# Edges between the stages of a two-block transformer kernel: what is split ahead, in which order tiles are summed, and where query blocks stand

## The chip, the cores and the metric

The kernel runs on one core of a Trainium2 chip. The metric is the device time of one execution in microseconds (us), the median of several runs. Five engines with a queue each work side by side and wait for each other by semaphores: TensorE (PE), VectorE (DVE), ScalarE (ACT), GpSimd (POOL), and SyncE (SP), which issues DMAs.

## The reference

Input x is one sequence of 512 tokens with 1024 features, all in fp32. The kernel holds it transposed, as 8 blocks of 128 features (partitions) by 512 tokens.

```python
# first block: gated linear attention and retention, 8 heads each
h = rms_norm(x, norm_g) * (1 + scale) + shift
m = sigmoid(ga) * uA + sigmoid(gb) * uB          # from h @ w_in, "mixed" in the kernel
x = rms_norm(x + gate * (m @ w_out), final_g)
# second block
def conformer_conv(x):
    a = glu(x @ w_pw1 + b_pw1)                   # 2048 columns
    y = depthwise_conv(a, w_dw, 31 taps, causal) + b_dw
    y = silu(layernorm(y, ln_g, ln_b))
    return y @ w_pw2 + b_pw2
h = x + conformer_conv(rmsnorm(x, norm_mix[0]))
h = h + swiglu_ffn(rmsnorm(h, norm_ffn[0]), up[0], down[0])
kv = rmsnorm(h, norm_kv) @ w_kv                  # 4 key/value heads of 64
q = rmsnorm(h, norm_mix[1]) @ w_q                # 16 heads, window of 128
h = h + banded_sink_attention(q, k, v, sinks, rel_bias) @ w_o
h = h + swiglu_ffn(rmsnorm(h, norm_ffn[1]), up[1], down[1])
out = rmsnorm(h, norm_final)
```

## The kernel before

**Dense layers.** Every weight matrix is cut into tiles of 1024 x 128 (one output block of 128 features). A tile is 512 KB. Tiles come in one long stream through four slots (`SLOTS`): SP loads tile n into `w_raw` (L429) when the low part of tile n-4 is made; ScalarE writes the high part `w_hi` (L557, `w_high`); GpSimd writes the low part `w_lo` = raw - high (L490, `w_low`). Inputs are split in the same way into `x_hi` and `x_lo`. Per block k of the input TensorE does three matmuls of 128x128 by 512: high with high, `w_hi` with `x_lo`, `w_lo` with `x_hi` (`dense`, L1445 to L1447), 24 a tile, into one PSUM bank of `gps`. The norm's factor is applied behind the matmul, so that a dense layer can start before the norm is known.

**Phases in order:** four pairs of heads (`pairs`, a hardware loop), `w_out`, `pw1` (16 tiles), the convolution, the layer norm, `pw2`, feed-forward 0, `kv`, `q` with the attention, `w_o`, feed-forward 1. `ahead(I, j)` on ScalarE makes the high part of the tile three further on than tile (I, j).

**w_out.** The last pair ends with `mix(0)` and `mix(1)` on VectorE, which write blocks 6 and 7 of `mixed` (L1185, L1187). ScalarE copies the 8 blocks to `xa_hi` (L741), GpSimd makes the low parts of blocks 0 and 1 (L503), VectorE those of 2 to 7 (L1218). `dense_behind` runs the first tile: 16 matmuls with the high input (L1457, L1458), then 8 with the low one (L1461). VectorE then expands the packed taps (`packs`, L1227).

**Residuals.** `residual` on VectorE, for each of 8 tiles: read tile c from PSUM and add it to `res` (L1252, L1254 or L1256), then add square c-1 into the running sum `lnv` (L1242; in w_out also a second sum into `hbuf`, L1245), then write low part c-1 of the next layer's input (L950). ScalarE's `residual`: the next high weight part (`ahead`), then for tile c the high part of the input (L586), the square (L759), in w_out a second, scaled square (L761). The sum over features is taken by TensorE with a matrix of ones: `sum_running` (L1506, L1507, in w_out also L1509, L1510), called behind the first tile of the next phase, at the end of the kernel behind the last tile. Behind w_out it gives two norms, since the first block's last norm and the second's first follow each other: ScalarE L768 to L774, VectorE L1272 and L1274 (`both_ready`).

**pw1 and the convolution.** VectorE scales each pair of tiles and gates them (`halves_in`, `gate`); it adds most taps (L1296), GpSimd 37 of them (L519) from ScalarE's products (L792), and TensorE does the last three chunks from packed taps (L1739) when SP has copied shifted rows (`spread`, L460). During pw1 ScalarE's queue also writes the relative bias to DRAM (L777, 3 MB). In the order of the programs, GpSimd waits for `both_ready` before the low part of pw1's tile 3, and ScalarE makes its high part in the loop over pw1.

**Layer norm.** TensorE adds up the means (`add_to_mean`, L1730), VectorE centers (L1328), ScalarE squares into two buffers in turn (L576), TensorE sums each square (L1500), two matmuls a sum; then ScalarE's logarithm and exponential (L581, L582), VectorE's scaling (L937), ScalarE's Silu in full precision (L830) and into `xa_hi` (L831), VectorE's low part (L943). `dense_abreast` starts pw2 on four tiles at once (L1472, L1473, L1478).

**Attention.** For each pair of heads c: scores (L1804), the minimum and exponential (L1387, L895), scaled probabilities (L1399), their transposes `band_probs(c, e)` (L1814), copies to `pT` (L881, L882), values (L1826). Between them TensorE does the query tile c+2 in parts of blocks (`queries`), and in the last two rounds parts of w_o's first three tiles (`out_part`). The output's high part is L887, its low part L1404.

Of the kernel before, what the change touches and what calls it, by code (L numbers as in the profile page):

```python
# [23 lines left out]
P = 128  # L24
T = 512
# [111 lines left out]
FIRST_LOW = 2  # L137
# [32 lines left out]
def program(nc, weights, ada_in, c_in, xT, x_turned, vec_in, sinks_in, rel_in, ret_tab, lvl_in, eye_in, tri_in, hot_in, ident_in, taps_in,  # L170
            rel_scratch, outT):
    ctx = ExitStack()
    with ctx:
# [68 lines left out]
        at_r = sb("at_r", [P, 2, 10 * P], where=first)  # L242
        first.close()
# [90 lines left out]
        m_hi = sem("m_hi")  # L334
        m_lo = sem("m_lo")
# [16 lines left out]
        center_done = sem("center_done")  # L352

# [47 lines left out]

        products = [hbuf[:, 0, :], hbuf[:, 1, :], hbuf[:, 2, :], sq[:, 0, :], sq[:, 1, :]]
# [79 lines left out]
        def _(pool):  # L482
            TT = nc.gpsimd.tensor_tensor
            for j in range(SLOTS):
                pool.sem_inc(lo_ready[j], 1)

# [9 lines left out]
            with pool.Fori(0, PAIRS) as p:  # L496
                for c in range(SLOTS - 1, PAIR_CHUNKS + SLOTS - 1):
                    if c not in GATE_CHUNKS:
                        w_low(p * (PAIR_CHUNKS // SLOTS) + (START["pairs"] + c // SLOTS), c % SLOTS)

            for c in range(FIRST_LOW):
                pool.wait_ge(m_hi, c + 1)
                TT(xa_lo[:, c, :], mixed[:, c, :], xa_hi[:, c, :].bitcast(F32), ALU.subtract).then_inc(m_lo, 1)  # L503
# [4 lines left out]
            for j in range(3):  # L508
# [17 lines left out]
            for n in range(3, 2 * KC):  # L526
# [15 lines left out]
            w_low(START["pw2"], 2)  # L542
            w_low(START["pw2"], 3)
# [6 lines left out]
        def _(act):  # L550
# [215 lines left out]
            residual("w_out", RMS_FIRST, lambda c: conv_gain[:, c:c + 1], xb_hi, lambda c: vcol("final_g", c))  # L766
            act.wait_ge(sum_done, SUMS[RMS_FIRST])
# [148 lines left out]
        def _(dve):  # L916
# [15 lines left out]
            def x_build(src, gain, hi, lo):  # L932
# [8 lines left out]
                for c in range(KC):  # L941
                    dve.wait_ge(xh_ready, KC * X_PW2 + c + 1)
# [291 lines left out]
            def residual(phase, n, scale=None, shift=None, build=None, double=False):  # L1234
# [13 lines left out]
                for c in range(KC):  # L1248
                    I, j = START[phase] + c // SLOTS, c % SLOTS
                    b = full(I, j)  # L1250
# [7 lines left out]
                    if c >= 2:  # L1258
# [779 lines left out]
```

## Time and profile before

| | |
|---|---|
| Median of 3 runs | 1688.26 us (1686.38 to 1688.56) |
| Profiled execution | 1689.8 us, its span 1688.0 us |
| Busy in the span | PE 1636.1, DVE 803.5, ACT 730.7, POOL 706.5 us |
| Mean granted TensorE clock | 0.989 |

The span goes from the first to the last instruction of the core. Times in the rows are us from its start. "Busy" counts the time in which an engine executes; the idle time of an engine that nobody waits for costs nothing.

### The profile page before, as it was taken

The page shows a single profiled execution, that of the slowest core. Times are in us where ns is not written, and L with a number is a line of the kernel's source. Part 1 is how long each engine was busy: PE and PEld are TensorE (multiplying, and loading weights), DVE is VectorE, ACT ScalarE, POOL GpSimd, SP SyncE. Part 2 cuts the span into 40 slices and gives each one's busy share as a digit, 9 for nine tenths or more (in the row PEclk, how much of TensorE's full clock was granted, in tenths as well). Part 3 has the DMA queues.
Part 4 walks back from the last instruction along what each step waited for, and adds up shares of the span by engine and source line. Part 5 has one row for each costly group of instructions (what it writes and reads, how often), then busy time and mean ns, then how long its engine had stood idle before and what let it go on. Part 6 is the DMA issues. An engine that isn't in the chain of part 4 may idle for free.

```text
span 1688.0 us, 22096 instructions
## 1 busy us (share of the span) xinstructions
PE 1636.1 (97%) x8056; PEld 1327.7 (79%) x8056; DVE 803.5 (48%) x1348; ACT 730.7 (43%) x1027; POOL 706.5 (42%) x303
## 2 busy tenths in 40 slices
PE   6999999999999999989999999999999999999997
PEld 4887887887878778647888888888787888888885
DVE  6684584584565758985321221235565321121123
ACT  4544554554554654454531222235665532222232
POOL 1353253343333437924444444444224444444432
PEclk9999999999999999999999999999999999999999
DMA  9321321331222337432233222233112323233221
GB/s 373 126 88 64 116 95 63 110 100 63 99 91 70 121 80 164 123 106 88 100 99 100 93 93 100 99 100 100 63 51 75 100 95 99 92 99 100 87 99 63
DMA packets 52324, 170.97 MB, mean 101 GB/s; under 512 B 5772, under 2 KB 10413, under 8 KB 51757
## 3 DMA queue, kind: packets, MB, share of 16 engines
q1 hardware_dynamic: 46000, 157.82, 28.0%
q10 hardware_dynamic: 6268, 12.39, 3.1%
q8 instruction: 38, 0.62, 0.1%
q14 instruction: 18, 0.14, 0.0%
HBM read 161.63 MB, written 5.24 MB: 99 GB/s over the span
## 4 chain that ended last, share of the span: by engine, by line
PE 84%; DVE 5%; issue 4%; ACT 3%; POOL 3%; SPq 1%; DMA 1%; ACTq 0%; DVEq 0%; POOLq 0%
PE gps L1445 23%; PE gps L1447 23%; PE gps L1446 22%; PE gps L1491 1%; POOL w_lo L490 1%; PE gps L1493 1%; PE gps L1492 1%; PE aps L1582 1%; POOL conv L519 1%; SPq L460 1%; PE aps L1654 1%; PE aps L1500 1%; PE gps L1739 1%; PE aps L1804 1%; PE aps L1660 1%
## 5 line engine op out<-in xcount | busy, mean ns | idle before, releaser
L490 POOL TENSOR_TENSOR w_lo<-w_raw,w_hi 128x1024 fp32r<-128x1024 f32 x260 | 656.3, 2527 | 943.4 <-ACT w_hi L557 943.2
L1445 PE MATMUL gps<-xa_hi,w_hi 128*128 128x512 f32 x1128 | 449.9, 399 | 5.2 <-DVE xa_lo L993 5.1
L1447 PE MATMUL gps<-xa_hi,w_lo 128*128 128x512 f32 x1128 | 440.0, 390 | 0.0
L1446 PE MATMUL gps<-xa_lo,w_hi 128*128 128x512 f32 x1128 | 439.7, 390 | 0.0
L557 ACT CAST w_hi<-w_raw 128x1024 fp32r<-128x1024 f32 x260 | 270.6, 1044 | 159.0 <-PE gps L1447 136.5
L1445 PE MATMUL gps<-xb_hi,w_hi 128*128 128x512 f32 x736 | 288.3, 392 | 3.0 <-POOL w_lo L490 1.8
L1447 PE MATMUL gps<-xb_hi,w_lo 128*128 128x512 f32 x736 | 286.5, 389 | 0.0
L1446 PE MATMUL gps<-xb_lo,w_hi 128*128 128x512 f32 x736 | 286.4, 389 | 0.0
L1445 PEld LDWEIGHTS gps<-xa_hi,w_hi 128*128 128x128 f32 x1128 | 212.0, 188 | 56.0 <-issue 6.9
L1446 PEld LDWEIGHTS gps<-xa_lo,w_hi 128*128 128x128 f32 x1128 | 212.2, 188 | 44.9 <-issue 3.1
L1447 PEld LDWEIGHTS gps<-xa_hi,w_lo 128*128 128x128 f32 x1128 | 212.0, 188 | 44.9
L1445 PEld LDWEIGHTS gps<-xb_hi,w_hi 128*128 128x128 f32 x736 | 138.1, 188 | 34.4 <-issue 3.3
L1447 PEld LDWEIGHTS gps<-xb_hi,w_lo 128*128 128x128 f32 x736 | 138.1, 188 | 28.9
L1446 PEld LDWEIGHTS gps<-xb_lo,w_hi 128*128 128x128 f32 x736 | 138.2, 188 | 28.8 <-issue 0.5
L1350 DVE TENSOR_TENSOR hbuf<-gps,rstd 128x512 f32<-128x512 f32 x44 | 30.4, 692 | 201.6 <-PE gps L1447 201.6
L1362 DVE TENSOR_TENSOR res<-gps,res 128x512 f32 x32 | 22.1, 692 | 142.8 <-PE gps L1447 142.8
L1349 DVE TENSOR_TENSOR sq<-gps,rstd 128x512 f32<-128x512 f32 x44 | 30.4, 692 | 119.6 <-PE gps L1447 104.5
L845 ACT ACTIVATE sq<-sq 128x512 f32<-128x512 f32 x44 | 27.8, 632 | 116.7 <-DVE sq L1349 116.6
L1296 DVE SCALAR_TENSOR_TENSOR aps<-glu,vec,aps 128x512 f32<-128x512 f32 x110 | 75.7, 748 | 0.7
L1491 PE MATMUL gps<-w_hi,xa_hi 128*128 128x256 f32 x256 | 73.3, 286 | 2.0 <-POOL w_lo L490 2.0
L1492 PE MATMUL gps<-w_hi,xa_lo 128*128 128x256 f32 x256 | 72.7, 284 | 0.0
L1493 PE MATMUL gps<-w_lo,xa_hi 128*128 128x256 f32 x256 | 72.7, 284 | 0.0
(253 smaller groups left out, 1879.9 us busy)
## 6 DMA issues: line engine op xcount, KB each, us to landing
w_raw<-weights_dram SPq DMA_DIRECT2D x268, 512.0 KB, 3.3
ada_w<-ada_in_dram SPq DMA_DIRECT2D x8, 1024.0 KB, 16.9
gates<-ret_tab_dram ACTq DMA_DIRECT2D x4, 1024.0 KB, 5.5
spread<-glu SPq DMA_DIRECT2D x48, 67.5 KB, 2.0
rel_scratch_dram<-rel_rows ACTq DMA_DIRECT2D x1, 3072.0 KB, 34.5
x<-x_turned_dram SPq DMA_DIRECT2D x2, 1024.0 KB, 8.2
res<-xT_dram ACTq DMA_DIRECT2D x1, 2048.0 KB, 8.9
bias<-rel_scratch_dram ACTq DMA_DIRECT2D x1, 2048.0 KB, 10.2
```

Of the source, the lines that this page charges most:

```text
L490: TT(w_lo[:, j, :], w_raw[:, j, :], w_hi[:, j, :].bitcast(F32), ALU.subtract).then_inc(lo_ready[j], 1)
L557: nc.scalar.copy(w_hi[:, j, :], w_raw[:, j, :]).then_inc(hi_ready[j], 1)
L845: nc.scalar.activation(sq[:, m, :], sq[:, m, :], ACT.Silu).then_inc(silu_ready, 1)
L1296: made_at[c] = own.mark(STT(bank, src, w, bank, ALU.mult, ALU.add))
L1349: TT(sq[:, m, :], full(I, 2 * m), rstd[:], ALU.mult).then_inc(evicted[2 * m], 1)
L1350: TT(h, full(I, 2 * m + 1), rstd[:], ALU.mult).then_inc(evicted[2 * m + 1], 1)
L1445: mm(gps[:, j, :], w_hi[:, j, w], x[0][:, k, :], start=k == 0, stop=False)
L1446: mm(gps[:, j, :], w_hi[:, j, w], x[1][:, k, :], start=False, stop=False)
L1447: last = mm(gps[:, j, :], w_lo[:, j, w], x[0][:, k, :], start=False, stop=k == blocks - 1)
L1491: mm(out, x[0][:, k, tok], wh, start=k == 0, stop=False)
L1492: mm(out, x[1][:, k, tok], wh, start=False, stop=False)
L1493: last = mm(out, x[0][:, k, tok], wl, start=False, stop=k == KC - 1)
```

## The change

It makes six groups of edits.

1. `lead`, a new buffer, takes the high and low part of block 0 of `mixed`, both made by GpSimd at the end of every pair behind `mix(0)` of that pair (the multiplication by 1 rounds to the high format). TensorE starts w_out with block 0 of tiles 0, 1 and 2, then the high parts of tiles 0 and 1, then their low parts, then tile 2. VectorE makes all eight low parts of the input.
2. The weights of pw1's tile 3 are split right behind w_out's squares on ScalarE, and on GpSimd ahead of its wait for `both_ready`.
3. In the layer norm the squares go to eight places (three of them used twice or shared with `sq`); GpSimd adds three pairs of them; TensorE takes five sums. The Silu into `xa_hi` comes ahead of the one in full precision.
4. In VectorE's `residual` the additions of squares and the low part of c-1 come ahead of the read of tile c, in all five residuals.
5. `sum_running` takes the running sum before it waits for the last square.
6. At the first pair of heads six query blocks instead of five stand before the first transposes; and the values of the last pair come ahead of tile 2 of w_o instead of behind its first four blocks.

```diff
@@ buffers, tables
+        lead = sb("lead", [P, 2, T], F32R, where=first)
+        ln_squares = [hbuf[:, c, :] for c in range(4)] + [sq[:, 0, :], sq[:, 1, :], hbuf[:, 1, :], hbuf[:, 3, :]]
-            SUMS[n] = SUMS.get(n - 1, 0) + (KC if n in (RMS_MIX, RMS_LN) else 1)
+            SUMS[n] = SUMS.get(n - 1, 0) + (KC if n == RMS_MIX else 1)
@@ gpsimd
+            pool.sem_inc(lead_ready, 1)
...
-            for c in range(FIRST_LOW):
-                pool.wait_ge(m_hi, c + 1)
-                TT(xa_lo[:, c, :], mixed[:, c, :], xa_hi[:, c, :].bitcast(F32), ALU.subtract).then_inc(m_lo, 1)
+                pool.wait_ge(mixed_ready, p * 2 + 2)
+                pool.wait_ge(lead_ready, p + 1)
+                TT(lead[:, 0, :], mixed[:, 0, :], ones[:, 0:1].to_broadcast([P, T]), ALU.mult).then_inc(lead_high, 1)
+                pool.wait_ge(lead_high, p + 1)
+                TT(lead[:, 1, :], mixed[:, 0, :], lead[:, 0, :].bitcast(F32), ALU.subtract).then_inc(lead_ready, 1)
+
             w_low(START["w_out"], 3)
...
-            for j in range(3):
+            for j in range(SLOTS):
                 w_low(START["pw1"], j)
...
             pool.wait_ge(both_ready, 1)
-            for n in range(3, 2 * KC):
+            for n in range(SLOTS, 2 * KC):
...
             w_low(START["pw2"], 2)
+            for i in range(3):
+                pool.wait_ge(sq_ready, KC * RMS_LN + 2 * i + 2)
+                a, b = ln_squares[2 * i:2 * i + 2]
+                TT(a, a, b, ALU.add).then_inc(pair_ready, 1)
             w_low(START["pw2"], 3)
@@ scalar
             residual("w_out", RMS_FIRST, lambda c: conv_gain[:, c:c + 1], xb_hi, lambda c: vcol("final_g", c))
+            ahead(START["pw1"], 0)
...
-                ahead(I, j)
+                if c > 0:
+                    ahead(I, j)
                 ahead(I, j + 1)
...
-                rms_square(RMS_LN, c, conv[:, c, :])
+                if c >= 6:
+                    act.wait_ge(pair_ready, c - 5)
+                nc.scalar.activation(ln_squares[c], conv[:, c, :], ACT.Square).then_inc(sq_ready, 1)
...
-                nc.scalar.activation(conv[:, c, :], hbuf[:, c % 4, :], ACT.Silu, bias=vcol("ln_b", c))
-                nc.scalar.activation(xa_hi[:, c, :], hbuf[:, c % 4, :], ACT.Silu, bias=vcol("ln_b", c))\
-                  .then_inc(xh_ready, 1)
+                nc.scalar.activation(xa_hi[:, c, :], hbuf[:, c % 4, :], ACT.Silu, bias=vcol("ln_b", c)).then_inc(xh_ready, 1)
+                nc.scalar.activation(conv[:, c, :], hbuf[:, c % 4, :], ACT.Silu, bias=vcol("ln_b", c)).then_inc(silu_done, 1)
@@ vector
-            dve.wait_ge(m_lo, FIRST_LOW)
-            for c in range(FIRST_LOW, KC):
+            for c in range(KC):
...
                 for c in range(KC):
                     I, j = START[phase] + c // SLOTS, c % SLOTS
+                    if c >= 2:
+                        add_squares(c - 1)
+                    if c >= 1 and build is not None:
+                        gain_low(build[0], c - 1, *build[1:])
                     b = full(I, j)
...
                     ins.then_inc(evicted[j], 1)
-                    if c >= 2:
-                        add_squares(c - 1)
-                    if c >= 1 and build is not None:
-                        gain_low(build[0], c - 1, *build[1:])
@@ tensor
+            def lead_block(I, slots):
+                pe.wait_ge(lead_ready, PAIRS + 1)
+                for j in slots:
+                    ready(I, j)
+                    mm(gps[:, j, :], w_hi[:, j, 0:P], lead[:, 0, :], start=True, stop=False)
+                    mm(gps[:, j, :], w_hi[:, j, 0:P], lead[:, 1, :], start=False, stop=False)
+                    mm(gps[:, j, :], w_lo[:, j, 0:P], lead[:, 0, :], start=False, stop=False)
...
                 pe.wait_ge(sq_used, USED[n] + KC - 2)
+                mm(aps[:, 0, :], ones[:], lnv[:], start=True, stop=False)
                 pe.wait_ge(sq_ready, KC * n + KC)
-                mm(aps[:, 0, :], ones[:], lnv[:], start=True, stop=False)
...
-            dense_behind(START["w_out"], 0, xa, lambda k: pe.wait_ge(m_hi, k + 1), lambda k: pe.wait_ge(m_lo, k + 1))
-            layer("w_out", xa, first=1)
+            lead_block(START["w_out"], (0, 1, 2))
+            dense_behind(START["w_out"], (0, 1), xa, lambda k: pe.wait_ge(m_hi, k + 1), lambda k: pe.wait_ge(m_lo, k + 1))
+            dense(START["w_out"], 2, xa, part=(1, KC))
+            layer("w_out", xa, first=3)
...
-            for c in range(KC):
-                sum_squares(RMS_LN, c)
+            for i, src in ((0, 0), (1, 2), (None, 6), (None, 7), (2, 4)):
+                if i is not None:
+                    pe.wait_ge(pair_ready, i + 1)
+                else:
+                    pe.wait_ge(sq_ready, KC * RMS_LN + src + 1)
+                last = mm(aps[:, 0, :], ones[:], ln_squares[src], start=i == 0, stop=i == 2)
+            last.then_inc(sum_done, 1)
...
-                queries(c + 2, 0, 5)
+                k0, k1 = (6, 7) if c == 0 else (5, 6)
+                queries(c + 2, 0, k0)
                 band_probs(c, 0)
-                queries(c + 2, 5, 6)
+                queries(c + 2, k0, k1)
                 band_probs(c, 1)
-                queries(c + 2, 6, KC)
+                queries(c + 2, k1, KC)
...
-            out_part(2, 0, 4)
             band_values(c)
-            out_part(2, 4, 7)
+            out_part(2, 0, 7)
```

`dense_behind` now takes the slots (0, 1) and the blocks 1 to 7: all high matmuls of both slots, then all low ones.

## Rows read from the trace of the kernel before

**Rows 1.** The page: busy time, share of the span and instructions of each engine

```profile
PE 1636.1 (97%) x8056; PEld 1327.7 (79%) x8056; DVE 803.5 (48%) x1348; ACT 730.7 (43%) x1027; POOL 706.5 (42%) x303
```

**Rows 2.** TensorE's waits: line, released by, us in total, times, longest

```profile
PE gps L1472 <- ACT xa_hi L831: 5.5, 1, 5.5
...
PE gps L1457 <- ACT xa_hi L741: 2.3, 2, 2.0
...
PE gps L1445 <- POOL w_lo L490: 1.8, 2, 1.3
...
PE aps L1814 <- DVE scores L1399: 1.4, 3, 1.0
PE gps L1445 <- issue: 1.2, 1, 1.2
```

**Rows 3.** Timeline at w_out's start: start, us, instruction, count, [idle before, releaser]

```profile
553.48 2.63 DVE L1187 TENSOR_TENSOR mixed<-gates 128x256 f32 x1
...
560.06 3.73 ACT L741 CAST xa_hi<-mixed 128x512 fp32r<-128x512 f32 x7
...
560.81 0.47 PE L1457 MATMUL gps<-xa_hi,w_hi 128*128 128x512 f32 x1 [1.98 <-ACT xa_hi L741]
...
562.72 1.52 DVE L1187 TENSOR_TENSOR mixed<-gates 128x256 f32 x1
...
564.37 3.70 DVE L1218 TENSOR_TENSOR xa_lo<-mixed,xa_hi 128x512 fp32r<-128x512 f32 x6
...
568.46 0.40 PE L1445 MATMUL gps<-xa_hi,w_hi 128*128 128x512 f32 x1
```

**Rows 4.** Timeline of VectorE in w_out's residual

```profile
573.82 1.40 DVE L1252 SCALAR_TENSOR_TENSOR res<-gps,mod,res 128x512 f32<-128x512 f32 x2
...
586.29 2.90 DVE L1245 TENSOR_TENSOR hbuf<-hbuf 128x512 f32<-128x512 f32 x1
589.12 2.87 DVE L950 SCALAR_TENSOR_TENSOR xb_lo<-res,conv_gain,xb_hi 128x512 fp32r<-128x512 f32 x1
...
601.35 0.75 DVE L1252 SCALAR_TENSOR_TENSOR res<-gps,mod,res 128x512 f32<-128x512 f32 x1 [1.57 <-PE gps L1447]
...
606.79 0.75 DVE L1252 SCALAR_TENSOR_TENSOR res<-gps,mod,res 128x512 f32<-128x512 f32 x1 [2.83 <-PE gps L1447]
```

**Rows 5.** Timelines of GpSimd and ScalarE in the same stretch

```profile
586.01 5.43 POOL L490 TENSOR_TENSOR w_lo<-w_raw,w_hi 128x1024 fp32r<-128x1024 f32 x2 [3.45 <-ACT w_hi L557]
...
603.28 0.71 ACT L761 ACTIVATE hbuf<-res,vec 128x512 f32<-128x512 f32 x1
...
605.01 2.38 POOL L490 TENSOR_TENSOR w_lo<-w_raw,w_hi 128x1024 fp32r<-128x1024 f32 x1 [2.98 <-ACT w_hi L557]
```

**Rows 6.** Timeline of ScalarE behind w_out's sums

```profile
616.66 0.69 ACT L768 ACTIVATE lnv<-aps,eps_col 128x512 f32<-128x512 f32 x1 [7.22 <-PE aps L1510]
```

**Rows 7.** Timelines of ScalarE and VectorE in pw1

```profile
647.79 1.05 ACT L557 CAST w_hi<-w_raw 128x1024 fp32r<-128x1024 f32 x1 [8.36 <-DMA w_raw<-weights_dram]
...
700.66 0.69 DVE L1305 TENSOR_TENSOR conv<-gps,lnv 128x512 f32<-128x512 f32 x1 [1.03 <-PE gps L1447]
```

**Rows 8.** Convolution and norm, timelines; last a stretch: busy of PE, PEld, DVE, ACT, POOL, clock, DMA

```profile
639.51 1.29 POOL L519 TENSOR_TENSOR conv<-conv,hbuf 128x512 f32<-128x512 f32 x1 [3.68 <-ACT hbuf L792]
...
732.27 4.88 DVE L1328 SCALAR_TENSOR_TENSOR conv<-aps,conv 128x512 f32<-128x512 f32 x8 [1.22 <-PE aps L1730]
...
739.39 1.99 PE L1500 MATMUL aps<-sq,ones 128*128 128x512 f32 x4
...
745.99 0.71 ACT L831 ACTIVATE xa_hi<-hbuf,vec 128x512 fp32r<-128x512 f32 x1
...
747.00:755.00 8.00, 8.00 (x27) 6.37 (x28) 7.44 (x12) 8.00 (x14) 0.00 (x0) 0.73 0.00 0
```

**Rows 9.** Timeline of ScalarE at the end of attention

```profile
1279.93 0.59 ACT L887 CAST xb_hi<-gps 128x512 fp32r<-128x512 f32 x1 [4.85 <-PE gps L1826]
```

**Rows 10.** Timeline of TensorE at the kernel's end

```profile
1675.34 1.10 PE L1506 MATMUL aps<-lnv,ones 128*128 128x512 f32 x2 [1.54 <-ACT sq L759]
```

More of the change, by code:

```diff
@@ L136 @@
 TURNED = (0, 2, 1, 3)
-FIRST_LOW = 2
 LAST_LOW = 2
@@ L334, in program @@
         m_hi = sem("m_hi")
+        lead_high = sem("lead_high")
+        lead_ready = sem("lead_ready")
         m_lo = sem("m_lo")
@@ L352, in program @@
         center_done = sem("center_done")
+        pair_ready = sem("pair_ready")
+        silu_done = sem("silu_done")
         s_full = sem("s_full")
@@ L941, in x_build @@
                 for c in range(KC):
-                    dve.wait_ge(xh_ready, KC * X_PW2 + c + 1)
+                    dve.wait_ge(silu_done, c + 1)
                     TT(lo[:, c, :], src[:, c, :], hi[:, c, :].bitcast(F32), ALU.subtract).then_inc(x_ready, 1)
@@ L1449, in dense, with dense_behind @@
                     last.then_inc(tile_done[j], 1)
-            def dense_behind(I, j, x, high, low):
-                ready(I, j)
-                for k in range(KC):
-                    high(k)
-                    w = slice(k * P, (k + 1) * P)
-                    mm(gps[:, j, :], w_hi[:, j, w], x[0][:, k, :], start=k == 0, stop=False)
-                    mm(gps[:, j, :], w_lo[:, j, w], x[0][:, k, :], start=False, stop=False)
-                for k in range(KC):
-                    low(k)
-                    last = mm(gps[:, j, :], w_hi[:, j, k * P:(k + 1) * P], x[1][:, k, :], start=False, stop=k == KC - 1)
-                last.then_inc(tile_done[j], 1)
+            def lead_block(I, slots):
[5 more added lines that the diff above has]
+                    mm(gps[:, j, :], w_lo[:, j, 0:P], lead[:, 0, :], start=False, stop=False)
+            def dense_behind(I, slots, x, high, low):
+                for j in slots:
+                    for k in range(1, KC):
+                        if j == slots[0]:
+                            high(k)
+                        w = slice(k * P, (k + 1) * P)
+                        mm(gps[:, j, :], w_hi[:, j, w], x[0][:, k, :], start=False, stop=False)
+                        mm(gps[:, j, :], w_lo[:, j, w], x[0][:, k, :], start=False, stop=False)
+                for j in slots:
+                    for k in range(1, KC):
+                        if j == slots[0]:
+                            low(k)
+                        last = mm(gps[:, j, :], w_hi[:, j, k * P:(k + 1) * P], x[1][:, k, :], start=False, stop=k == KC - 1)
+                    last.then_inc(tile_done[j], 1)
             def dense_abreast(I, x, high, low):
```

## The prediction

> **What bounds the kernel now.** First the page: TensorE is busy for 97% of the span [rows 1], so only its gaps can be won, and whatever lengthens a gap is paid in full. Then the waits of TensorE [rows 2]: the part of its idle time that these edits can reach is the start of w_out (2.3 us under L1457), two waits for a low weight part in pw1 (1.8), the gap before pw2 (5.5 under L1472), the first transposes of attention (1.4, of which 1.0 at head pair 0), and an "issue" gap of 1.2 in w_o. Then the timelines at these places.
>
> **Start of w_out.** TensorE begins tile 0 at 560.81, when ScalarE has copied block 0, and tile 1 only at 568.46; 24 matmuls take 5.44 us (read 6 to read 7 in [rows 4], both released by TensorE), so 2.2 us are lost here beside the gap. The change makes block 0 on GpSimd: `mix(0)` of the last pair ends at 556.1 [rows 3], two operations of 128x512 at about 1.3 (the conv addition in [rows 8]; L503's two took 1.6 each, which is the upper bound) give 558.9. Nine lead matmuls (2.05) reach 561.0; block k=1 is there at 561.2, ScalarE's copies come every 0.53 (seven in 3.73 from 560.06, [rows 3]), k=7 at 564.4. Two tiles' high parts end at 568.05, their 14 low matmuls at 571.25, tile 2 at 576.0, tile 3 at 581.5. Before, tile 2 ended at 568.46 + 2 x 5.44 = 579.3: TensorE is 3.4 us earlier. `mix(1)`, held at 562.72 for 1.52 by L503, ends near 562.45, and VectorE's eight low parts (0.62 each) end at 567.4. The same two GpSimd operations in pairs 0 to 2 cost nothing: its next weight part there comes several us later, and VectorE idles in those stretches.
>
> **The reordered residual.** This is where I expect the 3.4 us to be lost, and more. Before, VectorE took tile c from PSUM (the *read*, L1252) and then did the additions of squares c-1 and low part c-1. Now additions and low part come ahead of read c. In w_out each cycle becomes one closed chain: read c, ScalarE's copy and two squares, two additions, the low part, read c+1. And ScalarE's next instruction behind the squares is w_hi, which starts w_lo on GpSimd.
>
> The rows show what happens then. L1245 at 586.29 took 2.90 and L950 at 589.12 took 2.87, where the like take 0.62 to 0.75; they end 0.55 after GpSimd's operations, the second of which ended at 591.44 [rows 4, 5]. An operation of VectorE with two SBUF sources that starts while GpSimd works is held to the end. The read, with one source in PSUM, isn't.
> The cycle from rows: read to the end of the squares 601.35 to 603.99 = 2.64; GpSimd starts 1.02 later (605.01), at +3.66 [rows 4, 5]. The additions start at +2.68 and +3.3 (0.62 apart, [rows 3]), the low part at +3.9: 0.2 behind GpSimd. It is held for GpSimd's 2.65 (half of 5.43) and 0.5 more, so the next read starts at +6.8. TensorE makes a tile in 5.44.
>
> The Trainium skill says the same in "SBUF — State Buffer" (Who interferes with whom): with two SBUF inputs VectorE contends with a GpSimd instruction that reads SBUF, and whoever issues first keeps the port for the whole instruction. The trace agrees (2.90 and 2.87). By that rule the order of starts decides, and so both outcomes stand below.
>
> Step by step: read 0 at 573.3 (before 573.82; the weight expansion L1227 in front of it moves by half a us). Read 1 waits for low part 0: 0.78 + 0.72 + 0.65, at 575.45. Squares 1 stand behind w_hi 4 on ScalarE and end at 578.7; the first addition is held by w_lo 4 (to 579.35), the second by w_lo 5 (to 582.3); low part 1, then read 2 at 583.4. Read 3 at 590.15, reads 4 to 7 every 6.8, read 7 at 617.3, where before it was 606.79. The weights still come in time (w_lo 8 by 603.3). But the first tile of pw1 needs every low part: it starts at 603.5, stalls at k=5, 6 and 7, and has low part 7 at 617.3 + 0.78 + 0.72 + 0.65 = 619.5. A block of 0.68 and four sums of 0.86 (two sums take 1.99 less the 0.2 tail in [rows 8]) end at 623.6. The sums ended at 616.66 before [rows 6]: **+7.0**.
>
> After such idleness the granted clock falls to its half. Before pw2 TensorE idled 5.5 us, and the stretch behind it shows 0.73 [rows 8], which is some 4.3 us of 8 at 1.2 GHz, costing 2.2 us. Here two gaps of 3.5 and 6 us stand before the sums: I take the same **+2.2** (bounds: 0, and 4.0 if all 8 us ran at half).
>
> In the other residuals the same order does no harm: with one square the low part starts ahead of w_lo (3.3 us a cycle), and TensorE takes 4.08 or 5.44 per tile. After pw2 and w_o reads 2 to 4 come later (by up to 9 and 6 us), but tiles and weights have 3 us in hand.
>
> **pw1.** w_hi of pw1's tile 3 moves from behind the norm's chain to right behind the last square. ScalarE waits 7.22 for the sums there [rows 6], which hides the 1.05. The gap of 1.3 [rows 2] goes. The load into that slot is then issued before the 3 MB write of rel_scratch, not behind it: ScalarE's 8.36 of waiting for w_raw [rows 7] is now for the next tile, with the landing at the same time, so the second gap (0.5) goes too. VectorE idled 1.03 at the last tile of pw1 [rows 7] and from there sets the end of the taps; its reading of that tile follows TensorE: **-1.8** (bounds -1.0 and -2.5).
>
> **The norm.** Eight squares are no longer paced by TensorE: centerings come every 0.61 (eight in 4.88 from 732.27, [rows 8]), squares behind them from 733.0. GpSimd adds pairs (1.29, [rows 8]) at 734.3, 735.6 and 736.9; these don't hold the centerings, which read PSUM. TensorE's five sums follow at 735.6, 736.9, 737.8, 738.7, 739.5 and end at 740.35, against 741.38 [rows 8]: -1.0. The high Silu (L831) comes first, so the first block is there one Silu earlier; L831 takes 0.71 with its start-up ([rows 8]): -0.6. But TensorE now idles from 732.2 to 735.6, and a half clock for the sums would give 1.7 back. I take **-0.8** (bounds +0.3, -1.65). The weight part w_lo 3 of pw2, now behind the pair sums, is there at 740.7, before 745.
>
> **Attention and w_o.** At head pair 0 one more query block fills 0.68 of the 1.0; ScalarE's copies of the probabilities then hold the next scores: -0.25. In w_o the gap of 1.2 waits for w_lo 3 at the end of this chain: values 7, copy (1279.93), table, w_hi, w_lo. ScalarE had idled 4.85 before that copy [rows 9], so the probabilities were ready, and values 7, now four blocks (2.7 us) earlier, bring the whole chain forward. **-1.5** together (bounds -0.7, -1.9).
>
> **The end.** The last sum of squares 0 to 6 was held to 1675.34 for square 7 [rows 10]; it now runs ahead, and only one pair of matmuls is left behind square 7: **-0.9** (bounds -0.3, -1.1).
>
> Sum: 7.0 + 2.2 - 1.8 - 0.8 - 1.5 - 0.9 = **+4.2**. The profiled execution took 1689.8 (span 1688.0 and 1.8 around it), 1.5 above the median of 1688.26; 1694.0 on its scale, **1692.5** on the median's.
>
> **Rivals.**
> *A, the chain doesn't lock.* At w_out's residual the low part starts ahead of GpSimd, or GpSimd yields. For it: the margin is 0.2 us, and in other residuals L950 ran unheld in 0.74. Against it: both rows of [rows 4], where GpSimd started during an addition and took the next operation. The cycle is then 2.68 + 3 x 0.62 = 4.5, below 5.44: it decides at a cycle of 5.44. Read 3 is at 590.15 still, read 7 at 608.3, the sums end at 614.6: -2.0 instead of +9.2. Total -7.0: 1681.3, faster.
> *B, partly locked or cheaper clock.* The low part is held in some cycles only, or the clock stays at 2.4 GHz. Half the cycles held: read 7 at 612.8, the sums end 2.5 late; with -5.0 from the rest -2.5: 1685.8. All held and no clock loss, norm at its best: 7.0 - 5.9 = +1.1: 1689.4. Both are no change.
> *C, the lead block does nothing.* As VectorE's chain sets the end of w_out, the 3.4 us at its start don't count in my forecast at all; if GpSimd's broadcast multiply took twice 1.3, the time would be the same 1692.5. It is a rival only under A, where it would leave 1681.3 to 1682.6.
>
> **Chances.** Forecast 0.6, A 0.2 (C in it), B 0.2 (of that 0.04 beyond the 3.4 us on the fast side). What this kernel's measurement can tell from no change is about 0.2%, 3.4 us. Of the forecast's own range, 1690 to 1696, three quarters lie above 1691.7. Slower 0.6 x 0.75 = 0.45; within 0.15 + 0.16 = 0.31; faster 0.2 + 0.04 = 0.24. Range 1682 to 1696: it goes almost to A's time, and leaves out some two thirds of A and 0.05 above.
>
> **What would show it.** Right: in the profile after, L1252's reads 4 to 7 about 6.8 us apart, each behind an L950 of some 3 us; TensorE waiting for xb_lo (L950) in pw1's first tile by some 10 us in all; a granted clock below 1 near the sums. The gap in pw1, the 1.2 in w_o and one of the two sums' time at the end gone; tile 1 of w_out done near 571. Wrong: reads of w_out 5.44 apart and L950 at 0.74 there, which is A; or the five sums ending later than the eight did.

## The result and the profile after

The changed kernel takes 1691.06 us (median of 20 runs, 1688.62 to 1694.92) where the kernel before takes 1688.62 on the same chip (20 runs, 1685.77 to 1691.00): ratio 1.0015, 95% interval 1.0008 to 1.0022. It is slower, by 0.15% or 2.4 us, with the interval from 0.08% to 0.22%; the forecast was +4.2 with 1692.5. Its profiled execution took 1691.2 (span 1689.4), 1.4 more than that of before, so the stages below are compared with each other and not through the medians. In short: w_out became 8.65 us longer, and the other edits won less than that.

First the waits of TensorE after the change (line, released by, us in total, times, longest). Against [rows 2]: the start of w_out and both waits of pw1 for a low weight part are gone, as is the "issue" gap; L1814's 1.4 is L1847's 0.8. New are 8.2 us for the low parts of w_out's residual and 3.4 us for GpSimd's first pair of squares.

```profile
PE gps L1459 <- DVE xb_lo L965: 8.2, 3, 5.7
...
PE gps L1498 <- ACT xa_hi L846: 4.8, 1, 4.8
PE gps L1767 <- DMA spread<-glu: 4.3, 2, 3.0
...
PE aps L1794 <- POOL hbuf L554: 3.4, 1, 3.4
PE aps L1847 <- DVE scores L1413: 0.8, 3, 0.3
```

Then VectorE's timeline in w_out's residual (start, us, instruction, count, idle before and releaser), one cycle and the read that ends the next one; it answers to [rows 4]. A *read* is VectorE's taking of a tile from PSUM (L1270); L965 is the low part, L1256 and L1259 are the two additions.

```profile
592.46 0.74 DVE L1270 SCALAR_TENSOR_TENSOR res<-gps,mod,res 128x512 f32<-128x512 f32 x1
595.13 0.69 DVE L1256 TENSOR_TENSOR lnv<-lnv,sq 128x512 f32<-128x512 f32 x1 [1.93 <-ACT hbuf L773]
595.73 0.69 DVE L1259 TENSOR_TENSOR hbuf<-hbuf 128x512 f32<-128x512 f32 x1
596.34 2.89 DVE L965 SCALAR_TENSOR_TENSOR xb_lo<-res,conv_gain,xb_hi 128x512 fp32r<-128x512 f32 x1
599.15 0.74 DVE L1270 SCALAR_TENSOR_TENSOR res<-gps,mod,res 128x512 f32<-128x512 f32 x1
...
605.80 0.74 DVE L1270 SCALAR_TENSOR_TENSOR res<-gps,mod,res 128x512 f32<-128x512 f32 x1
```

And GpSimd's, which starts 0.23 us ahead of the low part, at 596.11 against 596.34, and ends 0.56 before it:

```profile
589.43 2.56 POOL L496 TENSOR_TENSOR w_lo<-w_raw,w_hi 128x1024 fp32r<-128x1024 f32 x1 [4.12 <-ACT w_hi L569]
596.11 2.56 POOL L496 TENSOR_TENSOR w_lo<-w_raw,w_hi 128x1024 fp32r<-128x1024 f32 x1 [4.12 <-ACT w_hi L569]
602.80 2.52 POOL L496 TENSOR_TENSOR w_lo<-w_raw,w_hi 128x1024 fp32r<-128x1024 f32 x1 [4.12 <-ACT w_hi L569]
```

The reads stand 6.69 us apart (592.46, 599.15) where a tile takes TensorE 5.44. No read waits for TensorE any more: the loop is VectorE, ScalarE, GpSimd, VectorE, and TensorE pays at pw1's first tile. The end of that tile, TensorE's timeline, and ScalarE's logarithm behind the sums (before 616.66, [rows 6]):

```profile
612.55 0.79 PE L1459 MATMUL gps<-xb_hi,w_hi 128*128 128x512 f32 x1 [5.66 <-DVE xb_lo L965]
...
616.27 1.91 PE L1531 MATMUL aps<-lnv,ones 128*128 128x512 f32 x2
617.97 1.83 PE L1533 MATMUL aps<-sq,ones 128*128 128x512 f32 x2
619.64 1.02 PE L1535 MATMUL aps<-hbuf,ones 128*128 128x512 f32 x2
...
621.56 0.69 ACT L781 ACTIVATE lnv<-aps,eps_col 128x512 f32<-128x512 f32 x1 [5.58 <-PE aps L1536]
```

Two sums' matmuls take 1.9 and 1.8 where the later two take 1.02: they run at 1.2 GHz (a granted clock of 0.50, "half clock" below) behind the 5.66 of idleness. The same stretch of both kernels, first before and then after (busy of PE, PEld, DVE, ACT, POOL, then the granted clock, DMA share, GB/s):

```profile
604.00:622.00 18.00, 18.00 (x72) 12.76 (x71) 4.43 (x7) 8.01 (x11) 2.38 (x1) 1.00 0.13 48
...
604.00:622.00 18.00, 9.82 (x21) 5.14 (x21) 8.44 (x8) 6.02 (x9) 6.17 (x3) 0.72 0.27 87
```

The layer norm after the change, timelines of VectorE, GpSimd, TensorE and ScalarE; it answers to [rows 8]:

```profile
735.66 4.88 DVE L1342 SCALAR_TENSOR_TENSOR conv<-aps,conv 128x512 f32<-128x512 f32 x8 [1.72 <-PE aps L1758]
...
737.69 2.51 POOL L554 TENSOR_TENSOR hbuf<-hbuf 128x512 f32<-128x512 f32 x2 [7.94 <-ACT hbuf L842]
...
739.02 5.40 PE L1794 MATMUL aps<-hbuf,ones 128*128 128x512 f32 x8 [3.40 <-POOL hbuf L554]
744.25 1.02 PE L1794 MATMUL aps<-sq,ones 128*128 128x512 f32 x2
...
745.31 0.69 ACT L593 ACTIVATE lnv<-aps,eps_col 128x512 f32<-128x512 f32 x1 [4.12 <-PE aps L1794]
```

The sums start where the forecast put them (3.36 behind the first centering, forecast 3.33) but eight of their ten matmuls take 5.40; stretches of 2 us show why:

```profile
739.00:741.00 2.00, 1.98 (x3) 0.90 (x4) 2.00 (x4) 2.00 (x4) 2.00 (x2) 0.52 0.30 107
741.00:743.00 2.00, 2.00 (x5) 0.78 (x4) 2.00 (x2) 0.20 (x1) 2.00 (x2) 0.63 0.00 0
743.00:745.00 2.00, 2.00 (x6) 0.73 (x4) 2.00 (x2) 0.00 (x0) 1.18 (x1) 1.00 0.00 0
```

**Stages of all kernels**, in us, each from one profiled execution. Their bounds are starts of instructions in the traces: the last pair's `mix(0)`; the first logarithm behind w_out's sums; VectorE's read of the last tile of pw1 ([rows 7] has it for before: 700.66); the logarithm of the layer norm; that of feed-forward 0's norm; that of the last norm. The six columns add up to the last start (before 1677.3, after 1678.7).

| | pairs | w_out | pw1 | taps and sums | pw2 | rest |
|---|---|---|---|---|---|---|
| before | 553.13 | 63.53 | 84.00 | 40.76 | 58.95 | 876.96 |
| after | 549.38 | 72.18 | 81.98 | 41.77 | 59.04 | 874.39 |
| e1 w_out's order back | 553.47 | 60.17 | 81.79 | 41.95 | 57.80 | 874.39 |
| e2 low part first | 552.38 | 60.22 | 81.84 | 42.88 | 58.95 | 874.40 |
| e3 no lead block | 552.94 | 72.95 | 81.85 | 41.30 | 57.62 | 874.40 |
| e4 before + order | 550.93 | 72.85 | 84.00 | 41.05 | 58.57 | 877.01 |
| e5 e1, no lead block | 549.11 | 63.48 | 81.88 | 42.51 | 57.81 | 874.39 |
| e6 e1, eight sums | 549.88 | 60.17 | 81.83 | 41.30 | 58.71 | 874.37 |
| e7 e6, old Silu order | 551.01 | 60.21 | 81.83 | 40.89 | 58.45 | 874.40 |
| e8 e1, pw1 weight late | 551.03 | 60.18 | 84.01 | 41.61 | 57.77 | 874.40 |
| e9 e1, six sums | 552.60 | 60.17 | 81.86 | 40.55 | 57.82 | 874.40 |
| e10 e1, attention, end back | 549.33 | 60.18 | 81.90 | 40.42 | 58.93 | 876.99 |

Three columns repeat to 0.2 us wherever the code is the same (w_out but for e3 and e4; pw1; rest). The pairs and the two stages around the layer norm scatter by 4.4, 2.5 and 1.4: differences in those three columns below these sizes are not readings of an edit by themselves.

A good part of this scatter is how long TensorE ran at half clock. In the pairs that was some 7 us in the four executions of 549.1 to 549.9 (after, e5, e6, e10), 10 in those of 551.0, 551.0 and 552.6 (e7, e8, e9), and 14 to 17 in the other five (550.9 to 553.5), which the change and the edits do not sort. In pw2 it is nearly all: take from the stage the way from the logarithm to the first matmul, and half of the time that TensorE then works at half clock, and 51.2 to 51.4 us are left in all twelve.

### The profile page after: what moved, and what is told of

Its sections match the earlier page's. It is cut to its first block, busy times and chain, and to the rows that moved or that the text cites. A ratio compares the mean times of both kernels' runs of the same rounds, so it can differ in the third digit from the quotient of the medians.

```text
span 1689.4 us, 22097 instructions
## 1 busy us (share of the span) xinstructions
PE 1632.0 (97%) x8050; PEld 1325.7 (78%) x8050; DVE 804.8 (48%) x1350; ACT 730.1 (43%) x1027; POOL 724.8 (43%) x312
## 4 chain that ended last, share of the span: by engine, by line
PE 81%; DVE 5%; issue 4%; ACT 4%; POOL 3%; SPq 2%; DMA 2%; ACTq 0%; DVEq 0%; POOLq 0%
PE gps L1459 22%; PE gps L1461 22%; PE gps L1460 21%; POOL w_lo L496 2%; SPq L465 2%; PE gps L1517 1%; PE gps L1518 1%; PE gps L1519 1%; DMA w_raw<-weights_dram 1%; POOL conv L527 1%; PE aps L1680 1%; PE aps L1837 1%; PE aps L1608 1%; PE aps L1686 1%; PE aps L1847 1%
## 5 line engine op out<-in xcount | busy, mean ns | idle before, releaser
L496 POOL TENSOR_TENSOR w_lo<-w_raw,w_hi 128x1024 fp32r<-128x1024 f32 x260 | 664.8, 2560 | 913.8 <-ACT w_hi L569 913.8
```

The lines of the kernel that those rows point to most:

```text
L496: TT(w_lo[:, j, :], w_raw[:, j, :], w_hi[:, j, :].bitcast(F32), ALU.subtract).then_inc(lo_ready[j], 1)
```

## The experiments

Each ran beside the kernel before: its median there was 1688.70 for e1 to e4 (14 runs), 1689.33 for e5 to e8 (14) and 1687.67 for e9 and e10 (15). The ratios are those on record; they are not the quotients of the two medians to the last digit (e7's median is 1.7 above e6's at the same ratio), so differences of 1 to 2 us between two experiments are taken from the stages.

**e1, w_out's order back.** The changed kernel; in w_out alone additions and low part stand behind the read again.

```diff
 for c in range(KC):
-    behind(c)          # additions of squares c-1, low part c-1
+    if not double: behind(c)
     b = full(I, j)     # ... read of tile c
+    if double: behind(c)
```

> The changed kernel, but in w_out's residual alone the additions of squares and low part c-1 stand behind the read of tile c again. If the locked chain there is the cause of the loss (theory): the last four reads follow TensorE's tiles 5.4 apart, no low part near them is held, TensorE has no wait for xb_lo in pw1's first tile, and the two gaps and the half clock behind them go: 12 us less than the changed kernel, 1679. If the loss comes from somewhere else, the norm or the loads in pw1 (rival): about 1691, with the 8 us of waits merely moved.

Measured: 1680.28 (6 runs), ratio 0.9948 [0.9935, 0.9961]. w_out takes 60.17 against 72.18, 12.0 less; the forecast had priced the reordering at 7.0 + 2.2 and the 3.4 swallowed, 12.6 in all. So the loss was the order in w_out, as the theory said. The timelines of VectorE and GpSimd show low parts of 0.74 in front of GpSimd's start and reads that wait for TensorE again:

```profile
591.39 0.74 DVE L965 SCALAR_TENSOR_TENSOR xb_lo<-res,conv_gain,xb_hi 128x512 fp32r<-128x512 f32 x1
591.62 2.77 POOL L496 TENSOR_TENSOR w_lo<-w_raw,w_hi 128x1024 fp32r<-128x1024 f32 x1 [1.30 <-ACT w_hi L569]
...
594.86 0.68 DVE L1259 TENSOR_TENSOR hbuf<-hbuf 128x512 f32<-128x512 f32 x1
595.46 0.74 DVE L965 SCALAR_TENSOR_TENSOR xb_lo<-res,conv_gain,xb_hi 128x512 fp32r<-128x512 f32 x1
...
596.56 2.40 POOL L496 TENSOR_TENSOR w_lo<-w_raw,w_hi 128x1024 fp32r<-128x1024 f32 x1 [2.18 <-ACT w_hi L569]
...
598.34 0.75 DVE L1275 SCALAR_TENSOR_TENSOR res<-gps,mod,res 128x512 f32<-128x512 f32 x1 [2.13 <-PE gps L1468]
```

The first two rows show the other direction: GpSimd's operation starts 0.23 behind a low part, which keeps its 0.74, and it is GpSimd's that takes longer, 2.77 against 2.40 where no such operation of VectorE runs.

**e2, low part first.** The changed kernel; everything still stands ahead of the read, but in w_out the low part goes ahead of the two additions, so that it starts well ahead of GpSimd's next operation and not 0.2 behind it.

```diff
+if double and c >= 1: gain_low(build[0], c - 1, *build[1:])
 if c >= 2: add_squares(c - 1)
-if c >= 1 and build is not None: gain_low(...)
+if c >= 1 and build is not None and not double: gain_low(...)
```

> The changed kernel, but in w_out's residual low part c-1 comes ahead of the additions of square c-1; everything still comes ahead of read c. Nothing is left out. If what counts is that the low part starts 0.2 us behind GpSimd and is held (theory): the low part now starts at +1.6, the additions at +2.7 and +3.3, both ahead of GpSimd at +3.7; the cycle is 4.0, below a tile's 5.4, and the time is within 2 us of e1_w_out_order_back, 1679 to 1681. If the closed chain itself is too long and the hold only a part of it (rival): the cycle gets 0.6 shorter, 6.1, and the time is 1688.

Measured: 1679.14 (6 runs), ratio 0.9939 [0.9926, 0.9952]; w_out 60.22, as e1. Its low part still overlaps the end of the previous GpSimd operation and takes 1.36, but the next one starts only 2.1 us later (593.60), and the additions are free of it:

```profile
589.57 2.72 POOL L496 TENSOR_TENSOR w_lo<-w_raw,w_hi 128x1024 fp32r<-128x1024 f32 x1 [1.30 <-ACT w_hi L569]
...
589.94 0.74 DVE L1272 SCALAR_TENSOR_TENSOR res<-gps,mod,res 128x512 f32<-128x512 f32 x1
591.48 1.36 DVE L965 SCALAR_TENSOR_TENSOR xb_lo<-res,conv_gain,xb_hi 128x512 fp32r<-128x512 f32 x1 [0.79 <-ACT xb_hi L598]
592.76 0.68 DVE L1256 TENSOR_TENSOR lnv<-lnv,sq 128x512 f32<-128x512 f32 x1
...
593.96 0.74 DVE L1272 SCALAR_TENSOR_TENSOR res<-gps,mod,res 128x512 f32<-128x512 f32 x1
```

The reads are 4.02 apart while they catch up with TensorE. So "ahead of the read" is not what costs, and the rival's cycle of 6.1 is out; it is that the low part starts behind GpSimd and waits for the whole operation.

**e3, no lead block.** The changed kernel with w_out's start of before (ScalarE's copy, GpSimd's low parts of blocks 0 and 1, one tile of `dense_behind`), and no `lead` in the pairs:

```diff
-TT(lead[:, 0, :], mixed[:, 0, :], ones[...], ALU.mult) ... # and the low part, every pair
-lead_block(START["w_out"], (0, 1, 2))
-dense_behind(START["w_out"], (0, 1), xa, ...)
-dense(START["w_out"], 2, xa, part=(1, KC))
+dense_behind(START["w_out"], 0, xa, ...)
```

> The changed kernel with the old start of w_out: no lead block, one tile's high part first, GpSimd makes two low parts. If VectorE's chain sets w_out's end and swallows the 3.4 us (theory): read 0 some 0.5 later at most, and the same time, 1691 to 1692, with TensorE's wait for xb_lo 3 us shorter. If the start still counts in full (rival): 1694.5.

Measured: 1693.98 (9 runs), ratio 1.0032 [1.0022, 1.0043]. In the trace w_out takes 72.95 against 72.18: the lead block gives 0.8 there, not 3.4 (1.0 at read 7; the sums of this execution spent less time at half clock). By the ratios it would be 0.0017, 2.9 us, with some 2 us of interval; the median lies nearer the rival's 1694.5, the trace nearer the theory, and between 0.8 and 2.9 these runs do not decide.

**e4, the order alone.** The kernel before with only the residuals reordered (the edit of e1 the other way, in all five residuals).

```diff
 for c in range(KC):
+    if c >= 2: add_squares(c - 1)
+    if c >= 1 and build is not None: gain_low(...)
     b = full(I, j)     # ... read of tile c
-    if c >= 2: add_squares(c - 1)
-    if c >= 1 and build is not None: gain_low(...)
```

> The kernel before with one edit of the change, the additions and the low part ahead of the read in all five residuals. Theory: reads 3 to 7 of w_out 6.7 apart, the sums behind w_out 9 us later, nothing won elsewhere: 1697.5. Rival (the order costs only together with the earlier start of w_out, which crowds the weights): within 1 us of before.

Measured: 1698.11 (6 runs), ratio 1.0054 [1.0039, 1.0069]: 9.1 us above before. Its w_out is 9.3 longer than before's (forecast 7.0 + 2.2 = 9.2), its reads are 6.69 apart (the last two, shown, 6.62). The order costs this by itself, without the earlier start:

```profile
608.34 0.74 DVE L1256 SCALAR_TENSOR_TENSOR res<-gps,mod,res 128x512 f32<-128x512 f32 x1
...
612.21 2.83 DVE L950 SCALAR_TENSOR_TENSOR xb_lo<-res,conv_gain,xb_hi 128x512 fp32r<-128x512 f32 x1
614.96 0.74 DVE L1256 SCALAR_TENSOR_TENSOR res<-gps,mod,res 128x512 f32<-128x512 f32 x1
```

Its pw1 and its rest are those of before (84.00, 877.01): in the three residuals that lie in the rest the order costs nothing and gives nothing. For that of pw2 (58.57 against 58.95) the scatter of its column leaves more room.

**e5, e1 without the lead block.** The edit of e3 in the kernel of e1.

> The kernel of e1 (w_out's additions and low part behind the read again: 1680.3, ratio 0.9948) without the lead block: w_out starts as in the kernel before, with ScalarE's copy of block 0, GpSimd's low parts of blocks 0 and 1, and one tile of dense_behind. Theory 1 (what the forecast worked out for the start: 3.4 us, swallowed only where VectorE's chain sets w_out's end): here nothing swallows it, so 1680.3 + 3.4 = 1683.7, read 7 of w_out some 50.7 us behind mix(0) as in the kernel before (606.79 - 556.1), where e1 has it some 47.3. Theory 2 (the lead block does little: what TensorE wins at tile 0 it loses again at the reads): at most 1.0 more than e1, 1680.3 to 1681.3.

Measured: 1684.58 (9 runs), ratio 0.9969 [0.9955, 0.9983]. w_out 63.48 against 60.17: the lead block is worth 3.3 here (3.5 by the ratios), as theory 1 said.

**e6, e1 with eight sums.** Squares in two buffers, eight sums, no pairs; the Silu into `xa_hi` stays first.

```diff
-nc.scalar.activation(ln_squares[c], conv[:, c, :], ACT.Square)
+rms_square(RMS_LN, c, conv[:, c, :])
-for i, src in ((0, 0), (1, 2), (None, 6), (None, 7), (2, 4)): ...
+for c in range(KC): sum_squares(RMS_LN, c)
```

> The kernel of e1 with the layer norm's squares back in two buffers and eight sums on TensorE, no pair additions on GpSimd; the Silu into xa_hi still comes first. In the changed kernel the logarithm of the layer norm stood 9.65 us behind the first centering (735.66 to 745.31), before 9.15 (732.27 to 741.42). Theory 1 (the five sums are the later ones, by 0.5 or more, and a half clock comes on top): 1679.5, at most 1680.0, with the logarithm 9.2 behind the first centering. Theory 2 (as I forecast: five sums are 1.0 earlier, and the 0.5 in the trace is chance): 1681.3, the logarithm still near 9.1 behind the centering, and e1's near 8.2 to 9.

Measured: 1680.49 (6 runs), ratio 0.9946 [0.9927, 0.9965], which the median can't tell from e1. In the trace the logarithm stands 9.16 behind the first centering. All eight-sum kernels have 9.15 or 9.16 (before, e4, e6, e7); the five-sum ones have 9.65 (after), 10.02 (e1), 9.44 (e2), 9.66 (e3), 10.64 (e5), 9.79 (e8) and, the exception, 8.33 (e10). The five sums are later in six of seven executions, by 0.3 to 1.5, and 0.8 earlier in the seventh. That is theory 1 in six and theory 2 in one; the stretches of e10 below show that the clock makes the difference.

**e7, e6 with the old order of the two Silus.**

> The kernel of e6 with the full-precision Silu first again, as before the change. Theory 1 (the order of the two Silus is worth one Silu, 0.35 to 0.6 us, in every run): 0.35 to 0.6 above e6, the first matmul of pw2 that much later behind the logarithm (5.07 in the changed kernel, 5.42 before). Theory 2 (pw2 is held by its weights or by the later blocks, and the order gives nothing): equal to e6 within 0.3 us, which the medians can't tell from theory 1; the distance from logarithm to first matmul decides.

Measured: 1682.21 (6 runs), ratio 0.9946 [0.9929, 0.9964]. From the logarithm to the first matmul of pw2 it takes 5.42 (before, e4, e7) against 4.80 or 4.81 (after, e1, e3, e6): 0.61 to the digit. But the stage pw2 is 58.45 here against 58.71 in e6. In e6 TensorE ran at half clock from 737.98 to 743.2, in e7 only from 739.36 to near 742.8 (0.55 in the stretch 741 to 743, 1.00 behind it): 5.3 us against 3.4, of which half, 0.9, is lost to e6. With that taken out, as below the table, 51.2 and 51.3 us are left behind the first matmul. So the 0.6 is there, theory 1, but in these two executions the clock covered it. Why the half clock lasted longer in e6 no run shows.

**e8, e1 with pw1's weight split late.**

```diff
-ahead(START["pw1"], 0)             # ScalarE, behind w_out's squares
-for j in range(SLOTS): w_low(...)  # GpSimd, ahead of both_ready
+for j in range(3): w_low(...)      # tile 3 in pw1's loop, behind both_ready
```

> The kernel of e1 with the early split of pw1's tile 3 undone (ScalarE makes its high part in the loop over pw1, GpSimd its low part behind the wait for both_ready). Theory 1 (forecast 1.8, trace 2.0 from the sums' logarithm to the last pair of pw1): 1680.3 + 1.9 = 1682.2, TensorE waits 1.3 and 0.5 for low weight parts in pw1 again. Theory 2 (the weights' wait takes the place of one for VectorE, which sets the end of the taps by itself): within 0.5 of e1, 1680.8 at most, the first centering no later.

Measured: 1681.88 (6 runs), ratio 0.9947 [0.9929, 0.9965]: no reading by itself. Its pw1 is 84.01 against 81.79, 2.2 us, and TensorE waits 1.7 for low weight parts there again, as theory 1 said.

**e9, e1 with six sums.** Squares 0, 1, 2 and 7 are summed singly, 3 and 4, 5 and 6 as pairs; squares 6 and 7 go to the places of 0 and 1.

```diff
-for i, src in ((0, 0), (1, 2), (None, 6), (None, 7), (2, 4)):
+for i, src in ((None, 0), (None, 1), (None, 2), (0, 3), (None, 7), (1, 5)):
-for i in range(3): ... # GpSimd: pairs (0, 1), (2, 3), (4, 5)
+for i in range(2): ... # GpSimd: pairs (3, 4), (5, 6)
```

> The kernel of e1 with six sums in the layer norm: squares 0, 1, 2 and 7 singly, squares 3 and 4 and squares 5 and 6 as pairs of GpSimd. Seen so far: with eight sums the logarithm starts 9.15 us behind the first centering (before, e4, e6, e7), with five 9.44 to 10.64, and with five TensorE waits 3.4 us for GpSimd's first pair, behind which half clock falls into the sums every time. Theory 1 (it is the 3.4 us of idleness that costs the five sums their gain): six sums start with square 0 at 1.4 behind the first centering, have no gap above 1.4 us, stay at full clock, end near 7.8 and the logarithm starts 7.8 to 8.1 behind the centering: 1.2 earlier than with eight sums and 2.0 earlier than e1's 10.0, so near 1678.5. Theory 2 (pair additions are late by themselves, each held behind VectorE or ScalarE, or the clock falls in the sums anyway): no better than eight sums, 9.1 or more, 1680.3.

Measured: 1677.03 (5 runs), ratio 0.9941 [0.9927, 0.9954]. The logarithm is 8.03 behind the first centering (727.15 to 735.18): TensorE never waits more than 1.45 us, and the clock is 1.00 through the sums (last two rows, stretches):

```profile
728.56 2.84 PE L1802 MATMUL aps<-hbuf,ones 128*128 128x512 f32 x6 [1.45 <-ACT hbuf L843]
732.30 1.98 PE L1802 MATMUL aps<-hbuf,ones 128*128 128x512 f32 x4 [0.90 <-POOL hbuf L555]
734.12 1.02 PE L1802 MATMUL aps<-sq,ones 128*128 128x512 f32 x2
...
735.18 0.69 ACT L594 ACTIVATE lnv<-aps,eps_col 128x512 f32<-128x512 f32 x1 [2.49 <-PE aps L1802]
...
732.00:734.00 2.00, 1.70 (x4) 0.71 (x5) 2.00 (x3) 0.69 (x2) 2.00 (x3) 1.00 0.00 0
734.00:736.00 2.00, 1.14 (x3) 0.31 (x2) 2.00 (x2) 0.81 (x2) 2.00 (x1) 1.00 0.00 0
```

That is theory 1. The kernel has the lowest median of all, 10.6 below the kernel before by its own, but not the lowest ratio (e2 has 0.9939); by the intervals it can't be told from e1, e2, e6, e7 or e8. That it is the fastest is not shown; that its norm is the shortest is, in one execution.

**e10, e1 with the attention's and the end's edits undone.**

```diff
-k0, k1 = (6, 7) if c == 0 else (5, 6)
+k0, k1 = (5, 6)
-band_values(c); out_part(2, 0, 7)
+out_part(2, 0, 4); band_values(c); out_part(2, 4, 7)
 pe.wait_ge(sq_ready, KC * n + KC)   # ahead of the running sum again
```

> The kernel of e1 with two edits undone: the query block and the values of the last pair of heads stand as in the kernel before, and the last sum of squares waits for the last square before it takes the running sum. Theory 1 (the forecast's terms, 1.5 for attention and w_o and 0.9 for the end): 1680.3 + 2.4 = 1682.7; TensorE's gap of 1.2 in w_o is back, and from the end of feed-forward 0 to the logarithm of the last norm it takes 2.4 us more than e1. Theory 2 (only the end counts; what attention wins is lost again to w_o's weights): 1680.3 + 0.9 = 1681.2, no gap of 1.2 in w_o, 0.9 in the trace behind the last tile.

Measured in the trace: rest 876.99 against 874.39, 2.6 us, and the two waits are back (TensorE's list):

```profile
PE aps L1539 <- ACT sq L771: 1.5, 1, 1.5
PE aps L1854 <- DVE scores L1420: 1.4, 3, 1.0
PE gps L1466 <- issue: 1.2, 1, 1.2
```

That is theory 1, in the stages. e10 also has the five sums, and its execution is the one in which the clock stayed at 1.00 through them, behind the same 3.40 of idleness (TensorE's timeline, then two stretches):

```profile
726.86 4.08 PE L1801 MATMUL aps<-hbuf,ones 128*128 128x512 f32 x8 [3.40 <-POOL hbuf L554]
...
727.00:729.00 2.00, 1.89 (x4) 0.64 (x5) 2.00 (x4) 2.00 (x4) 2.00 (x2) 1.00 0.07 26
729.00:731.00 2.00, 2.00 (x6) 0.95 (x5) 2.00 (x2) 0.04 (x1) 2.00 (x2) 1.00 0.00 0
```

The eight matmuls take 4.08 where they took 5.40 after the change, and the logarithm is 8.33 behind the centering (723.50 to 731.83), 0.8 earlier than with eight sums. The medians say more: 1684.72 (11 runs), ratio 0.9983 [0.9974, 0.9992], 0.0035 or 5.9 us above e1, with some 2.7 either way. The profiled execution (1680.2) was the shortest of the eleven, and it is one that kept the clock in the sums; what the other ten lost has no trace, and that part stays open. The clock alone is not it: at a mean granted clock of 0.991, e10's five runs took 1684.3 to 1685.2 and e1's one run 1679.9.

## Why the prediction was right, point by point

**w_out: +9.2 forecast, +8.65 measured.** The mechanism was the one forecast in each of its parts: the low part starts 0.23 behind GpSimd (forecast 0.2), takes 2.89 (forecast 2.9), the cycle is 6.69 (6.8), read 7 is 63.0 behind `mix(0)` (617.3 - 553.13 = 64.2), the sums run at half clock. Forecast were 2.2 for that; measured are 2.4 (the first sum to the logarithm takes 5.29 against 3.63 in e1, and the block of pw1's first tile just ahead of it 1.44 against 0.69). The cycle is a tenth shorter than forecast because GpSimd's operation takes 2.56 here and not 2.65. Of the three runs that change only the order, e1 and e4 move w_out by 12.0 and 9.3, and e2 shows that the loop opens when the low part starts well ahead of GpSimd's next operation. Rival A, the loop that doesn't lock, had 1681.3; e1 and e2, where it doesn't, took 1680.3 and 1679.1. TensorE's wait for low parts is 8.2, forecast some 10.

The Trainium skill's "SBUF — State Buffer" (Who interferes with whom) gives the rule that whoever issues first holds the port for its whole instruction. The traces agree in both directions: 2.89 for the low part that starts second, and in e1, where it starts 0.23 first, 0.74 for it and 2.77 for GpSimd's operation. What the runs add is how much hangs on it: which of the two is first, here by 0.2 us, makes 12 us of w_out. How small a shift would turn it no run tested.

**The lead block, swallowed.** 0.8 in the locked loop by the trace (e3), 3.3 in the open one (e5), where the forecast had 0 and 3.4. The 0.8 is a small error: the loop's first reads still follow TensorE's start, read 0 coming 19.7 behind `mix(0)` (forecast 20.2) with the lead block and 20.7 without it (e3).

**pw1: -1.8 forecast, -2.02 measured**, and 2.2 in e8. Both waits are gone.

**The norm: -0.8 forecast, +1.1 measured** (taps, sums and pw2: 99.71 before, 100.81 after). This step failed. The forecast subtracted 1.0 for five sums and kept the 1.7 of a half clock as a bound; the runs show the bound in six executions of seven. TensorE idles 3.4 us until the first pair, matmuls behind it run at 1.2 GHz, and the logarithm comes 0.3 to 1.5 later than with eight sums. Adding the 1.7 to the forecast's own -1.0 gives +0.7, in the middle of these; in e10, where the clock stayed, it is -0.8, the forecast's term nearly. The second term, -0.6 for the Silu, is exact at the first matmul (e6 and e7); behind it TensorE spent 6.0 us at half clock after the change and 4.4 before, and half of the difference is 0.8. So both terms were right or nearly so, and the step that failed is the clock, left out of the middle value: the +1.1 lies outside the stated bounds (+0.3, -1.65), and one of the forecast's own signs of being wrong, the five sums ending later than the eight, is met. What the clock does shows from the first centering to feed-forward 0's logarithm (68.10 before, 68.70 after), beside the mean granted clock of the 24 us from that centering on:

| | granted clock | us |
|---|---|---|
| eight sums: before, e4, e6, e7 | 0.86 | 67.6 to 68.1 |
| five sums: e1, e3, e8, e10 | 0.86 | 67.3 to 67.8 |
| five sums: after, e2, e5 | 0.79 | 68.4 to 68.7 |
| six sums: e9 | 0.93 | 65.85 |

Over all seven the five sums average 67.9, and the eight 67.8: by these runs the edits of the norm are worth nothing on average, and 0.3 where the clock is the same. Of the +1.1, 0.5 lie before the first centering (31.61 behind pw1's last tile before, 32.12 after). That distance is 31.74 in e7 and 33.44 in e2 with the same taps, so it is no reading of the change.

**Attention, w_o and the end: -2.4 forecast, -2.57 measured** (876.96 to 874.39), the same in every kernel that has the edits. A late read of VectorE in feed-forward 1 (1645.26 before, 1647.59 after, so +2.3, where the logarithm of feed-forward 0's norm had +4.0 and the last one +1.4) parts it into -1.7 and -0.9; forecast -1.5 and -0.9.

**The sum.** 8.65 - 2.02 + 1.10 - 2.57 = +5.2 behind the pairs; the pairs took 3.75 less in this execution than in that of before, with some 7 us at half clock in them against 17 (kernels with and without the change's work there have both), which leaves the 1.4 between the two executions. The forecast of +4.2 lacked 1.9 at the norm and had 0.9 too much in the other terms; the medians differ by +2.4. That gap of 2.8 is within the scatter of the pairs: one profiled execution tells stages, not totals. The mechanism of the largest term was forecast and is shown; that the total came as near as it did is in part luck, since the errors of the norm and of the other terms have opposite signs and the medians moved by less than the stages.

## What to carry to other kernels

Before moving an operation on VectorE with two SBUF inputs, write down when it and its neighbour on GpSimd start in the new order, to a tenth of a us: if GpSimd is first, the operation waits for all of GpSimd's (2.89 us where 0.74 is usual), and a loop through both engines can lock at a period above TensorE's (6.69 against 5.44). Fewer instructions on the busiest engine are no gain if it idles for them first: mix direct and paired terms so that it always has one to do (e9), and price the slower clock behind every idle stretch you add. A gain at a stage's start is only worth what is left at its end: the lead block, the early split, the attention and the end gave 3.3 + 2.2 + 2.6 = 8.1 us in e1, of which the lead block's 3.3 shrank to 0.8 where the loop locked; the other two stood in their stages all along, and the total hid them. Look at stages before you judge an edit by the median.

## What the runs showed of the hardware that I had not expected

The stretch at 1.2 GHz follows the idleness, not the work: from the first centering to pw2 there was one before, behind the logarithm; with a 3.4 us gap added in front of the sums a second one fell into the sums, in six executions of seven (not in e10, for no reason that the traces show; never in the five that lack the gap), and the one at pw2 stayed (0.50 at 751 to 755 after, at 746 to 750 before). And nearly the same code up to the last `mix(0)` took 549.1 to 553.5 us in these executions; three of the five above 552 (before, e1, e9) have a wait of 2.7 us for `packed` there, the others none above 1.6. This scatter is larger than every edit but one, and it goes with the clock: of the 20 runs of the changed kernel the five at a mean granted clock of 0.991 took 1688.6 to 1689.5 us, the six at 0.987 or 0.988 took 1691.3 to 1694.9.
